# Even mixer: projections of q, k and v in halves between the SSD units, and other PSUM banks for the first turn of the normed output

## The reference: what is computed

```
proj = rms_norm_2(x, mix_norm) @ w_in
q, k, v, z, xbc, dt_raw = jnp.split(proj, EVEN_SPLITS, axis=-1)
q = rms_norm_2(q per head);  k = rms_norm_2(k per head)
na_out = neighbourhood_attention(q, k, v, na_rel_bias)
xbc = jax.nn.silu(centred_depthwise_conv(xbc, conv_w, conv_b))
xs, bm, cm = split(xbc)
y_fwd = ssd_scan(xs, dt[:, :, 0], A[0], bm, cm)
y_bwd = flip(ssd_scan(flip(xs), flip(dt[:, :, 1]), A[1], flip(bm), flip(cm)))
y = y_fwd + y_bwd + D_skip[:, None] * xs
ssd_out = gated_group_rms_norm(y, z, out_norm)
return jnp.concatenate([na_out, ssd_out], axis=-1) @ w_out
```

## Time and profile before

| | us |
|---|---|
| median of three runs | 1731.02 |
| lowest and highest of them | 1730.76 and 1738.96 |
| the profiled execution | 1739.91 |
| its span, first to last instruction | 1738.5 |
| TensorE busy | 1667.5 (96%) |
| VectorE, ScalarE busy | 975.3 (56%), 786.7 (45%) |
| mean granted clock of TensorE | 0.972 |

### The profile page before, as it was taken

The page is one execution under the profiler, slowest core; times in us unless marked ns, Lnnn a source line. Parts: engine busy times, 40 slices in busy tenths (PEclk is TensorE's granted clock), DMA queues, the critical chain, the costliest instruction groups (busy, mean ns, idle before and its releaser), DMA issues. The chain is left out here.

```text
span 1738.5 us, 18632 instructions
## 1 busy us (share of the span) xinstructions
PE 1667.5 (96%) x7938; PEld 1360.0 (78%) x7938; DVE 975.3 (56%) x992; ACT 786.7 (45%) x954; POOL 68.6 (4%) x99
## 2 busy tenths in 40 slices
PE   6999998999999999998999999999999998599999
PEld 5877776788888888797788879877788886378887
DVE  5646665554555454745554467766554557544543
ACT  5444544443444344544444357533443444534342
POOL 1000000100000000000000010100000002000000
PEclk9999998999999999999999999978999999699999
DMA  8454441454555553633545463313454543026451
GB/s 337 180 184 180 189 152 59 156 208 173 202 184 195 184 201 146 236 147 124 204 180 193 170 229 146 146 39 84 178 199 181 202 174 146 1 106 226 176 193 49
DMA packets 51391, 289.33 MB, mean 166 GB/s; under 512 B 14151, under 2 KB 14791, under 8 KB 18026
## 3 DMA queue, kind: packets, MB, share of 16 engines
q1 hardware_dynamic: 50732, 286.84, 45.0%
q10 hardware_dynamic: 576, 1.29, 0.2%
HBM read 287.06 MB, written 1.05 MB: 166 GB/s over the span
## 5 line engine op out<-in xcount | busy, mean ns | idle before, releaser
L1760 DVE TENSOR_TENSOR wl<-raw,wh 128x2048 fp32r<-128x2048 f32 x260 | 588.7, 2287 | 157.2 <-ACT wh L1146 157.2
L516 PE MATMUL ps<-wh,xTh 128*128 128x512 f32 x1408 | 561.2, 399 | 19.6 <-DVE wl L1760 8.4
L516 PE MATMUL ps<-wh,xTl 128*128 128x512 f32 x1408 | 554.3, 394 | 0.0
L516 PE MATMUL ps<-wl,xTh 128*128 128x512 f32 x1408 | 553.8, 393 | 0.0
L1146 ACT ACTIVATE wh<-raw 128x2048 fp32r<-128x2048 f32 x260 | 488.8, 1907 | 3.8 <-PE ps L516 2.6
L516 PEld LDWEIGHTS ps<-wh,xTh 128*128 128x128 f32 x1408 | 268.0, 190 | 84.9 <-DVE xTl L1799 10.6
L516 PEld LDWEIGHTS ps<-wh,xTl 128*128 128x128 f32 x1408 | 267.5, 190 | 57.3
L516 PEld LDWEIGHTS ps<-wl,xTh 128*128 128x128 f32 x1408 | 268.0, 190 | 54.4
L2452 POOL TENSOR_SCALAR st<-st 128x1 f32<-128x1 f32 (+2 forms) x46 | 29.4, 640 | 1482.0 <-ACT tmp L1165 850.3
L1209 ACT ACTIVATE sgf<-ps,st 128x256 f32<-128x256 f32 x22 | 10.4, 474 | 104.1 <-PE ps L516 104.1
L1209 ACT ACTIVATE sge<-ps,st 128x256 f32<-128x256 f32 x22 | 10.4, 474 | 98.9 <-PE ps L516 98.9
(11 more groups left out here) (330 smaller groups left out, 2298.9 us busy)
## 6 DMA issues: line engine op xcount, KB each, us to landing
raw<-in_w SPq DMA_DIRECT2D x260, 1024.0 KB, 4.8
gains<-in_rows SPq DMA_DIRECT2D x18, 512.0 KB, 4.0
x<-in_x ACTq DMA_DIRECT2D x2, 512.0 KB, 7.7
nab<-in_rpb SPq DMA_DIRECT2D x32, 32.0 KB, 2.5
out_x<-x SPq DMA_DIRECT2D x2, 512.0 KB, 2.6
qn<-in_rpb SPq DMA_DIRECT2D x16, 32.0 KB, 2.5
xd<-in_rpb SPq DMA_DIRECT2D x16, 32.0 KB, 2.6
df<-in_cst SPq DMA_DIRECT2D x1, 368.0 KB, 23.3
```

Of the source, the lines that this page charges most:

```text
L516: return pe.matmul(o, lhs, rhs, start=start, stop=stop, skip_group_check=False)
L1760: TT(wl[:, p % RAW, :], raw[:, p % RAW, :], wh[:, p % RING, :].bitcast(F32), ALU.subtract).then_inc(*lo(p))
```

## The change

`project` can do one of its two halves alone (`parts`). q, k and v are projected in halves, `qk_half` and `v_half`, which stand between the units of the scan in TensorE's order; the three engines' orders are rewritten to fit. On TensorE `qk_turn(1, 1, 6)` now comes after `decays(7)`, v's last half after `outputs(5)`. The first turn of the normed output uses banks 0 and 1 in place of 6 and 7. SyncE's and POOL's programs are as they were.

```diff
--- before.py
+++ after.py
@@ -525,13 +525,14 @@
                     m = pe.transpose(bank(b)[:, width * k:width * k + 128], s, ident[:, :])
                 return m
 
-            def project(name, p, t, b, emptied_by, act=(xTh, xTl), bias=None, mid=None):
+            def project(name, p, t, b, emptied_by, act=(xTh, xTl), bias=None, mid=None, parts=(0, 1)):
                 on.wait_ge(act_lo, name, t, 1)
-                clear(b)
-                emptied[b] = [emptied_by]
+                if 0 in parts:
+                    clear(b)
+                    emptied[b] = [emptied_by]
                 if bias is not None:
                     mm(bank(b), ones2[:, :], bias, True, False)
-                for half in range(2):
+                for half in parts:
                     on.wait_ge(*split_of(p + half))
                     H, L = hi_part(p + half, 4), lo_part(p + half, 4)
                     for k in range(4):
@@ -870,8 +871,8 @@
                     m.then_inc(*formed("cb", t))
                     emptied[b] = emptied[b + 1] = [(copied, "cb", t)]
 
-                def qk_part(j, t):
-                    project("evenmix", p0 + 12 + 2 * j, t, 6 + t, (made, "qk", j, t))
+                def qk_half(j, t, half):
+                    project("evenmix", p0 + 12 + 2 * j, t, 6 + t, (made, "qk", j, t), parts=(half,))
 
                 def qk_turn(j, t, b):
                     on.wait_ge(made, "qk" if j else "qkg", j, t)
@@ -923,12 +924,12 @@
                     m.then_inc(*formed("off", l))
                     emptied[0] = emptied[1] = [(product, "off", l)]
 
-                def v_part(t):
-                    project("evenmix", p0 + 16, t, 6 + t, (copied, "vn", t))
+                def v_half(t, half):
+                    project("evenmix", p0 + 16, t, 6 + t, (copied, "vn", t), parts=(half,))
 
                 def turn_ssd(l):
                     on.wait_ge(made, "ssd_out", l)
-                    b0 = 2 if l else 6
+                    b0 = 2 * l
                     for b in range(2):
                         clear(b0 + b)
                         transposes(b0 + b, [xn[:, l, 512 * b + 128 * k:512 * b + 128 * k + 128] for k in range(4)]).then_inc(*flipped("ssd", l, b))
@@ -997,38 +998,44 @@
                 group(2)
                 group(3, sums)
                 state_products(0)
-                qk_part(0, 0)
+                qk_half(0, 0, 0)
                 state_products(1)
+                qk_half(0, 0, 1)
                 x_turn(0)
-                qk_part(0, 1)
+                qk_half(0, 1, 0)
                 x_turn(1)
                 decays(0)
+                qk_half(0, 1, 1)
                 qk_turn(0, 0, 5)
-                qk_part(1, 0)
                 decays(1)
-                qk_turn(0, 1, 5)
+                qk_half(1, 0, 0)
                 outputs(0)
                 crossing(0)
-                qk_part(1, 1)
+                qk_turn(0, 1, 5)
                 decays(2)
+                qk_half(1, 0, 1)
                 outputs(1)
-                v_part(0)
                 decays(3)
+                qk_half(1, 1, 0)
                 outputs(2)
-                qk_turn(1, 0, 7)
-                v_part(1)
+                qk_half(1, 1, 1)
                 decays(4)
                 outputs(3)
+                v_half(0, 0)
                 crossing(1)
+                decays(5)
+                qk_turn(1, 0, 7)
+                v_half(0, 1)
+                outputs(4)
+                turn_ssd(0)
+                decays(6)
+                v_half(1, 0)
+                outputs(5)
+                v_half(1, 1)
+                decays(7)
                 qk_turn(1, 1, 6)
-                decays(5)
-                outputs(4)
-                decays(6)
-                outputs(5)
-                turn_ssd(0)
-                decays(7)
+                out_ssd(0, 0)
                 outputs(6)
-                out_ssd(0, 0)
                 scores(0)
                 outputs(7)
                 out_ssd(1, 0)
@@ -1554,7 +1561,7 @@
                     for b in range(2):
                         on.wait_ge(flipped, "ssd", l, b)
                         on.wait_ge(multiplied, p0 + 17)
-                        act.activation(xTh[:, 4 * b:4 * b + 4, l, :], halves((2 if l else 6) + b), ACT.Copy).then_inc(*act_hi("ssd", l, b))
+                        act.activation(xTh[:, 4 * b:4 * b + 4, l, :], halves(2 * l + b), ACT.Copy).then_inc(*act_hi("ssd", l, b))
 
                 def scores(i):
                     P, a = hood_P(i), 12 * (i % 3)
@@ -1628,38 +1635,38 @@
                 ring.need(p0 + 14)
                 ring.fill(1, p0 + 12)
                 gate(3, 1)
+                state_products(1)
                 qk_stat(0, 0)
-                state_products(1)
                 factors()
                 x_turn(0)
                 ring.fill(1, p0 + 12)
-                qk_stat(0, 1)
                 x_turn(1)
                 decays(0)
+                qk_stat(0, 1)
                 ring.need(p0 + 16)
                 qk_turn(0, 0, 5)
+                decays(1)
                 ring.fill(1, p0 + 13)
+                qk_turn(0, 1, 5)
+                decays(2)
+                ring.fill(1, p0 + 14)
                 qk_stat(1, 0)
-                decays(1)
-                qk_turn(0, 1, 5)
-                ring.fill(1, p0 + 14)
-                qk_stat(1, 1)
-                decays(2)
+                decays(3)
                 ring.need(p0 + 18)
                 ring.fill(1, p0 + 15)
-                v_part(0)
-                decays(3)
-                qk_turn(1, 0, 7)
+                qk_stat(1, 1)
+                decays(4)
                 ring.fill(1, p0 + 16)
-                v_part(1)
-                decays(4)
-                ring.fill(1, p0 + 17)
-                qk_turn(1, 1, 6)
                 group_squares(0)
                 decays(5)
+                qk_turn(1, 0, 7)
+                v_part(0)
+                turn_ssd(0)
                 decays(6)
-                turn_ssd(0)
+                ring.fill(1, p0 + 17)
+                v_part(1)
                 decays(7)
+                qk_turn(1, 1, 6)
                 ring.fill(1, p0 + 18)
                 ring.need(p0 + 22)
                 scores(0)
@@ -2234,7 +2241,7 @@
                     for b in range(2):
                         on.wait_ge(act_hi, "ssd", l, b)
                         u = slice(4 * b, 4 * b + 4)
-                        TT(xTl[:, u, l, :], halves((2 if l else 6) + b), xTh[:, u, l, :].bitcast(F32), ALU.subtract).then_inc(*act_lo("ssd", l, b))
+                        TT(xTl[:, u, l, :], halves(2 * l + b), xTh[:, u, l, :].bitcast(F32), ALU.subtract).then_inc(*act_lo("ssd", l, b))
 
                 def scores(i):
                     P, B, a = hood_P(i), hood_bias(i), 12 * (i % 3)
@@ -2308,43 +2315,43 @@
                 steps_x(0)
                 qk_scale(0, 0)
                 ring.fill(1, p0 + 12)
+                steps_x(1)
+                entering(0)
+                weigh(0)
                 qk_sum(0, 1)
-                steps_x(1)
-                weigh(0)
+                ring.need(p0 + 16)
                 qk_scale(0, 1)
-                ring.need(p0 + 16)
-                entering(0)
+                weigh(1)
+                entering(1)
                 ring.fill(1, p0 + 13)
-                qk_sum(1, 0)
-                weigh(1)
-                qk_scale(1, 0)
-                entering(1)
-                ring.fill(1, p0 + 14)
                 crossed(0)
                 steps_x(2)
-                qk_sum(1, 1)
                 weigh(2)
+                ring.fill(1, p0 + 14)
+                qk_sum(1, 0)
+                steps_x(3)
+                qk_scale(1, 0)
+                weigh(3)
                 ring.need(p0 + 18)
-                qk_scale(1, 1)
-                ring.fill(1, p0 + 15)
-                steps_x(3)
-                weigh(3)
-                ring.fill(1, p0 + 16)
                 skipped(0)
                 steps_x(4)
+                ring.fill(1, p0 + 15)
+                qk_sum(1, 1)
+                qk_scale(1, 1)
+                gated(0)
                 weigh(4)
-                gated(0)
+                steps_x(5)
                 crossed(1)
-                steps_x(5)
+                normed(0)
                 weigh(5)
-                normed(0)
+                ring.fill(1, p0 + 16)
+                turn_ssd(0)
                 steps_x(6)
                 weigh(6)
+                steps_x(7)
+                skipped(1)
                 ring.fill(1, p0 + 17)
-                turn_ssd(0)
-                steps_x(7)
                 weigh(7)
-                skipped(1)
                 ring.fill(1, p0 + 18)
                 ring.need(p0 + 22)
                 scores(0)
```

## The result

The changed kernel takes 1739.40 us (median of 20 executions, 1735.83 to 1743.76); the kernel before, on the same chip in turn, 1730.91 us (20 executions, 1725.32 to 1738.96). The ratio is 1.0052 with a 95% interval of 1.0038 to 1.0066: slower by half a per cent. I had forecast 1728.6 us and a range up to 1738.0, so the time lies 10.8 us above the forecast and 1.4 us above the range, and of my three cases the one with the chance of 0.09 came. I go by the ratios.

What follows compares the result with a forecast made beforehand. TensorE's half clock in the even stage was taken as the bound. Gain of 4.9 us, limited by bias loads, less 1.65 and 0.8 clock losses gave -2.4 us, off the 1731.02 median: 1728.6 us; eight in ten 1721.5 to 1738.

Steps and rivals of the forecast that it cites:

- my three cases: Whole kernel against before: faster by over 0.5% (chance 0.10), within 0.5% (0.81), slower by over 0.5% (0.09).
- The wait before `decays(7)`: TensorE waits 1.75 us for ScalarE's exponential, queued behind copies that wait for v's last half projection.
- The loads back to back behind `qk_turn(1, 1)`: SyncE's four groups of 16 bias loads follow each other from 1162.6, limiting the full-clock gain to 4.9 us.
- Full recovery of the clock: Even stage: half-clock stretches on TensorE cost 13.6 us in the first three and 3.5 us in the fourth.
- the anchor: Start of state_products(0) in the even stage, 1089.34 in the old trace, from which the new order was laid out.
- the stretches that I had given 0.8 us: Half a chance of one more half-clock stretch ahead of 1162.5, moving the chain of loads by 1.65 us: 0.8 us.
- I take the same difference off the median: Last step: the 2.4 us gain under the profiler, subtracted from the median of three runs, 1731.02, gives 1728.6 us.
- The sum of -2.4 us: Net change under the profiler: -4.9 gain, +1.65 and +0.8 for clock losses; ends -4.9 and +1.9.
- Before is already fast: Unprofiled before keeps its clock in this stage while loads hold the new order: slower by 5.7 to 6.4 us; chance 0.27.
- The loads don't bind: The 64 bias loads go faster than 10.5 us a group, so 12.6 us of gain shows: 1718.5 us; chance 0.08.
- The clock falls anyway: Half projections too short; four 3.3 us half-clock stretches remain ahead of 1162.5: +4.2 us, 1735 us; chance 0.10.
- Clock by busy share alone: Half-clock falls with TensorE busy stay, 13.6 us, and delay the loads: about +10 us, 1741 us; chance 0.05.

Runs made afterwards that it cites:

- e10_before_banks: The kernel before, with only the first turn of the normed output put in banks 0 and 1: 1729.78 us, ratio 0.9983 to before.
- e9_exp_first_only: The changed kernel, with the exponentials of decays(6) ahead of turn_ssd(0) on ScalarE and VectorE's steps to match: 1738.59 us, ratio 1.0031 to before.
- e6_before_again: The kernel before, unedited, profiled once more: 1730.09 us.
- e5_before_again: The kernel before, unedited, profiled once more: 1726.22 us.
- e4_before_loads_late: The kernel before, with the first group of bias loads waiting for decays(7) instead of the last turn of k: 1738.78 us, ratio 1.0032 to before.
- e1_turn_early: The changed kernel, with qk_turn(1, 1) moved ahead of outputs(4) and into bank 7: 1728.19 us, ratio 0.9987 to before.
- e3_loads_merged: The changed kernel, with the same bias bytes in 8 loads a group instead of 16: 1734.12 us, ratio 1.0000 to before.
- e7_before_merged: The kernel before, with the same bias bytes in 8 loads a group instead of 16: 1735.79 us, ratio 1.0003 to before.
- e2_early_and_exp: The changed kernel, with qk_turn(1, 1) ahead of outputs(4) and the exponentials of decays(6) ahead of turn_ssd(0): 1728.85 us, ratio 0.9985 to before.
- e11_second_order: The changed kernel with early turn, exponentials first, 8 loads a group, out_ssd(3, 0) before scores(2), ScalarE's turn(1, 0) copy before its exponentials: 1723.80 us, ratio 0.9940 to before.

## Why the prediction was wrong, point by point

**What was right.** The wait before `decays(7)`: 1.75 us forecast, 1.72 measured, released by ScalarE as written. The loads back to back behind `qk_turn(1, 1)`, and `scores(0)` on VectorE waiting for them (5.78 us). `scores(2)`: 4.4 us forecast, 4.62 measured; TensorE's arrival there and the release both came some 4 us later than laid out, so the size of this wait is in part luck. No wait ahead of `turn_ssd(0)` or `qk_turn(1, 0)`, so these two were rightly costed at nothing. The banks: nothing, as e10_before_banks shows. Full recovery of the clock: I worked out 13.6 + 3.5 = 17.1 us from the half-clock stretches, and before with the clock kept has a stage 15.6 us shorter (144.6 - 129.0), its own 1.02 us wait included. The halves did keep the clock through the units where before mostly loses it.

**What was off in size.** `qk_turn(1, 1)` ended 76.7 us after the anchor (1168.04 - 1091.34) instead of 73.2. The half projections don't wholly hold the clock, which was to stay near 1.00 up to 1162: in `outputs(3)` it fell for 4 us at 0.59, which lost 1.6 us (e9_exp_first_only has the same fall, the other five kernels with this order up to there don't). Behind the new wait it fell again, within `decays(7)`: this unit and `qk_turn(1, 1)` took 3.3 us up to the next start instead of 2.5. These are the stretches that I had given 0.8 us. Another 0.3 us is that the turn's transposes end later than the next unit starts, and 0.7 us remain, mostly from units a little longer than the ones I laid out. Every load is 3.5 us later for it: the third group ended its issue 108.65 us after the anchor, where I had 105.2. The waits of 2.4 us before `scores(1)` and 4.3 us before `turn(1, 1)` came out at 0.79 and none, since TensorE at half clock (1165 to 1172.5, 1193 to 1203.5) filled the same time with work; e9_exp_first_only, with the clock kept from 1150 to 1175, has them at 3.43 and 3.48. `out_ssd(0, 1)` starts 116.2 us after the anchor, against 112.0 to 114.7 forecast and 116.9 in before. So under the profiler the stage gained 0.6 us where I had 2.4: inside my ends of -4.9 and +1.9.

**The step that failed** is the last one: "I take the same difference off the median." The sum compares two orders against one execution of before, and that execution was one of the slowest third of before's; in its trace the clock is at half for 34 us. The median execution of before, 1730.91 us, lies with e6_before_again, which has 14 us at half clock and a stage of 135.3 us, and a good quarter of the executions lie with e5_before_again at 129.0. The new order can't follow them there, because its loads hold the stage: the three traces with late loads (after, e4_before_loads_late, e9_exp_first_only) have 142.1 to 144.0 us, and the quickest execution of the changed kernel, 1735.83 less 1594 to 1600 for all else, leaves 136 to 142. The sum of -2.4 us was thus off by 2 us against the execution that it was made from (the stage gained 0.6), and by more than ten against those at 1726 and 1730. The prediction names this as its last sign of being wrong: that the unprofiled runs of before keep the clock where the profile lost it.

**The rival that came true** is *Before is already fast*. Mechanism and place are as written there: the old order reaches `out_ssd(0, 1)` early, the new one is held by the loads. What it lets before win, 8.9 us from the profiled execution to the median, was right (9.0 with the 20 executions). Its price of 5.7 to 6.4 us was 8.5, since `out_ssd(0, 1)` came 116.2 us after the anchor where this rival has 113.6 to 114.4, behind loads that were 3.5 us late. Its chance of 0.27 was the second error: I set "one run is at 1738.96 and two at 1731" against stretches at half clock elsewhere, though those two to one were the best evidence at hand on how often the profiled case occurs, and though all else in the program turned out to take the same time within 6 us. Even that rival's 1737 us lies within 0.5% of before, so I left only 0.09 for slower; with its price a third higher it crossed that line.

*The loads don't bind* fell for the changed kernel (e1_turn_early, e3_loads_merged, e4_before_loads_late) and holds for before as far as its times tell (e7_before_merged). *The clock falls anyway*: in the main no. Ahead of the loads there were some 6 us at half clock and not four stretches of 3.3; in the stage it went from 34 to 20 us, with e2_early_and_exp and e11_second_order at none. But 20 us is no less than the 14 us of e6_before_again, because half of it lies behind the wait of 4.62 us. *Clock by busy share alone*: TensorE was busy for all of the 7.5 us from 1165 at 0.57, and busy for all of the 17.0 us at 0.50 in one execution of before and at 1.00 in another. The Trainium skill, TensorE: Matmul & The Clock Gate, Part 1, says that activity releases the throttle. This trace and these runs don't agree with that as far as it is read as busy or idle, and they don't show what else decides.

**What stays open.** Why the clock falls for longer in some executions of before than in others, and in e5_before_again not at all, with the same instructions in the same order. What can be said is where: in the units of `decays` and `outputs`, above all where several follow each other without a projection, and behind waits. The 1.7 us wait before `decays(7)` had half clock behind it in all three traces that have it (after, e1_turn_early, e3_loads_merged), and so had the waits of 4.62, 4.52, 3.48 and 3.43 us; the 2.0 us wait before `scores(2)` had it in one of two, the wait of 2.75 us in e2_early_and_exp had none. Only single profiled executions stand behind this, so it is a pattern and not shown as a cause. Open, too, is how much of the 11 us that e1_turn_early brings is the waiting itself and how much the clock behind it (7 us of half clock in the stage instead of 20).

## What to carry to other kernels

When the gain of a change is to come out of the clock, first see how the unprofiled times of the kernel before are spread, or profile it two or three times: where they fall into groups, work out the change against each group and weigh the results, and don't take the profiled one's difference off the median. A step that is moved on TensorE for the clock's sake is to be followed down to what it releases; here four transposes put ten microseconds later started a chain of 64 small loads that takes 42 us, and took away the quick executions that the old order has. A gain shows only when the last such floor is off: halves, early turn, exponential first and half the loads gave nothing against before until one wait on VectorE was covered with work, and then the whole kernel was 0.6% faster than before.

## What the runs showed of the hardware

The same program took 1724.5 to 1743.0 us, in three groups that occur in every set of executions taken together; one trace from each shows TensorE's clock at half in this stage for none, 14 and 34 us, and the stage at 129.0, 135.3 and 144.6 us. Issuing a small load costs SyncE's queue 0.65 us at 32 KB and at 64 KB alike: 8 loads of 64 KB took 5.3 us where 16 of 32 KB had taken 10.4. The landing did change: 4.8 us after the issue in e3_loads_merged. The Trainium skill, DMA: Bandwidth & Descriptors, Anatomy of one DMA, puts a fixed cost of about 2.0 us on a DMA issued from GpSimd, which no run here shows; the 32 KB loads from SyncE landed 2.5 us after their issue, but in a chain of many it was the time of issue that counted.
